# Expert blocks of 32 slots, four side by side, in a two-layer diffusion backbone on one NeuronCore

## The reference

```python
scores = jax.nn.sigmoid(jnp.dot(t, router_w))          # 16 experts in 4 groups
sel = scores + router_b                                # group of the best two sums, then top 2 inside it
a = jnp.einsum('td,edf->tef', t, w_gate)               # (1024 -> 256) per expert
b = jnp.einsum('td,edf->tef', t, w_up)
act = jax.nn.silu(a) * b * gates[:, :, None]           # gates: the two normalised scores, 0 elsewhere
return jnp.einsum('tef,efd->td', act, w_down)          # (256 -> 1024)
```

## Time and profile before

| | |
|---|---|
| Runs | 1114.5, 1116.32, 1115.82 us; median 1115.82 |
| Profiled execution | span 1112.5 us from first to last instruction; no time of its own beside the span |
| TensorE | busy 1058.8 us, 95% of the span |
| VectorE, ScalarE, GpSimd | 572.7, 389.0, 204.8 us |
| DMA | 241.47 MB, mean 217 GB/s |

### The profile page before, as it was taken

The page is one execution under the profiler, slowest core; times in us unless marked ns, Lnnn a source line. Parts: engine busy times, 40 slices in busy tenths (PEclk is TensorE's granted clock), DMA queues, the critical chain, the costliest instruction groups (busy, mean ns, idle before and its releaser), DMA issues.

```text
span 1112.5 us, 17990 instructions
## 1 busy us (share of the span) xinstructions
PE 1058.8 (95%) x5918; PEld 589.1 (53%) x5919; DVE 572.7 (51%) x1223; ACT 389.0 (35%) x800; POOL 204.8 (18%) x313
## 2 busy tenths in 40 slices
PE   3999999999999899999999999899999979999996
PEld 0566564555544455555546655555644445555552
DVE  0334545665345754454574545476724674534557
ACT  0332224444211244444333222454511134444540
POOL 0133456000000100100152435800000011001003
PEclk9999999999999999999999999999999999999999
DMA  9940006668801799999981000557540379999917
GB/s 351 361 138 1 1 9 238 217 222 302 331 19 40 248 378 377 381 358 366 332 289 41 1 1 0 187 194 279 207 149 38 112 260 376 381 379 380 376 78 284
DMA packets 129064, 241.47 MB, mean 217 GB/s; under 512 B 12304, under 2 KB 92192, under 8 KB 122864
## 3 DMA queue, kind: packets, MB, share of 16 engines
q1 hardware_dynamic: 115904, 194.83, 50.1%
q0 software_dynamic: 7056, 25.69, 6.3%
q10 hardware_dynamic: 6048, 20.22, 4.5%
HBM read 213.63 MB, written 27.10 MB: 216 GB/s over the span
## 4 chain that ended last, share of the span: by engine, by line
PE 80%; DMA 8%; DVE 3%; issue 3%; SPq 3%; POOL 1%; ACT 1%; DVEq 0%; POOLq 0%; ACTq 0%
PE bank L1120 17%; PE pair L1045 12%; PE pair L1160 9%; PE pair L762 7%; PE pair L777 6%; DMA big<-ada_w 4%; PE pair L895 4%; PE pair L794 3%; PE bank L811 3%; PE bank L931 3%; PE bank L672 3%; PE pair L1090 3%; PE bank L910 2%; PE bank L746 2%; DMA big<-y_rows,big 2%
## 5 line engine op out<-in xcount | busy, mean ns | idle before, releaser
L1120 PE MATMUL bank<-big,actT 128*64 (+1 forms) x928 | 206.3, 380 | 2.4 <-ACT actT L1445 1.9
L1120 PE MATMUL bank<-actT 128*64 128x256 f32 x928 | 206.5, 381 | 0.0
L1120 PEld LDWEIGHTS bank<-big,actT 128*64 128x64 f32 x928 | 124.7, 137 | 83.1 <-issue 26.0
L1045 PE MATMUL pair<-big,actT 128*128 128x512 f32 x320 | 142.7, 598 | 0.0
L1120 PEld LDWEIGHTS bank<-actT 128*64 128x64 f32 x928 | 124.7, 137 | 0.0
L1160 PE MATMUL pair<-big 128*64 (+1 forms) x464 | 106.0, 598 | 0.7 <-ACT big L1470 0.7
L1045 PEld LDWEIGHTS pair<-big,actT 128*128 128x128 f32 x320 | 59.0, 190 | 67.8 <-issue 67.6
L762 PE MATMUL pair<-big,actT 128*128 128x384 f32 (+1 forms) x320 | 93.6, 447 | 0.3 <-ACT actT L1218 0.2
L1988 DVE TENSOR_REDUCE mx<-pair 128x1 f32<-128x640 f32 x64 | 52.7, 823 | 72.0 <-PE pair L896 71.9
L1642 POOL DMA_INDIRECT big<-h_rows,big x29 | 27.7, 956 | 304.3 <-PE pair L1090 286.9
L762 PEld LDWEIGHTS pair<-big,actT 128*128 128x128 f32 x320 | 59.5, 190 | 29.3 <-ACT actT L1218 1.9
(11 more groups left out here) (274 smaller groups left out, 1628.9 us busy)
## 6 DMA issues: line engine op xcount, KB each, us to landing
big<-ada_w SPq DMA_DIRECT2D x48, 1024.0 KB, 5.0
big<-w_gate SPq DMA_DIRECT2D x32, 1024.0 KB, 13.1
big<-w_up SPq DMA_DIRECT2D x32, 1024.0 KB, 16.3
big<-w_down SPq DMA_DIRECT2D x32, 1024.0 KB, 14.5
y_rows<-big ACTq DMA_DIRECT2D x28, 512.0 KB
big<-w_out SPq DMA_DIRECT2D x4, 2048.0 KB, 13.4
big<-mod_rows SPq DMA_DIRECT2D x16, 512.0 KB, 9.2
h_rows<-big ACTq DMA_DIRECT2D x10, 512.0 KB, 2.7
```

The costliest lines, as they stand in the source:

```text
L1045: m = mm(dst, actT[:, k, t * P:(t + 1) * P], vw.wo[n][:, k, :], start=(k == order[0]), stop=(k == order[-1]))
L1120: m = mm(dst[CH * h:CH * h + CH, 0:DE], xgT[:, k, CH * h:CH * h + CH], weights(h, k * 2 * DE + lo, DE), start=(k == 0), stop=(k == DC - 1) ...
```

## The change

Blocks have 32 slots (`CH`), and four of them (`NPART`) stand side by side in a step, each on 32 columns of the array. Block 0 still reads the ring. Blocks 1 to 3 read copies, which now pass through queues of three pieces each: the 6144 columns of an expert are six pieces of 1024 (gate 0 and 1, up 2 and 3, down 4 and 5), and piece `i` of block `c` stands in `parts[c][i % 3]`. `ACT_TAKES` and `DVE_TAKES` say which engine copies which blocks of each piece. One semaphore, `used`, counts the pieces that TensorE is done with, and takes the place of `gu_mm` and `dn_mm`. Step 0 of a layer holds blocks of expert 0 alone and reads the ring for all four. The copies of pieces 0 to 2 of a step stand in the step before it, those of 3 to 5 in the step itself, so each engine reads places twice a step. Gate and up weights lie in the ring as runs of 8 KB (rows `8p` to `8p+7` in partition `p`), and so `norm2` writes its rows in the matching order. Every expert gets at least one block, expert 0 at least four. The SBUF set aside for DMA descriptors shrinks to 4096 bytes a partition.

```diff
-CH = 64
-NSTEP = 18
+CH = 32
+NPART = P // CH
+NSTEP = 15
+PIECE = D
+NPIECES = 6
+ACT_TAKES = [(1, 3), (1,), (1,), (1, 3), (1,), (1,)]
+DVE_TAKES = [(2,), (2, 3), (2, 3), (2,), (2, 3), (2, 3)]
...
+        fifo = sb("fifo", [P, 3 * PIECE])
...
-                    sp.dma_start(wgu[s][:, :, 0:DE], w_gate[l, e].rearrange("(k p) n -> p k n", p=P)).then_inc(ld_w[s], 16)
-                    sp.dma_start(wgu[s][:, :, DE:2 * DE], w_up[l, e].rearrange("(k p) n -> p k n", p=P)).then_inc(ld_w[s], 16)
+                    sp.dma_start(wg[s], w_gate[l, e].rearrange("(p k) n -> p (k n)", k=DC)).then_inc(ld_w[s], 16)
+                    sp.dma_start(wu[s], w_up[l, e].rearrange("(p k) n -> p (k n)", k=DC)).then_inc(ld_w[s], 16)
...
+                def weights_of(n, place, i):
+                    if n is not None:
+                        w_a, w_d = w_s
+                        pe.wait_ge(w_a, n * ACT_STEP + sum(len(t) for t in ACT_TAKES[:i + 1]) - 1)
+                        pe.wait_ge(w_d, n * DVE_STEP + sum(len(t) for t in DVE_TAKES[:i + 1]) - 1)
...
+                    for i in range(4):
+                        weights = weights_of(None if first else n, place, i)
+                        dst = (tb4, tb5)[i // 2]
+                        for k in range(4 * (i % 2), 4 * (i % 2) + 4):
+                            for c in range(NPART):
+                                m = mm(dst[CH * c:CH * c + CH, 0:DE], xgT[:, k, CH * c:CH * c + CH],
+                                       weights(c, k % 4 * DE, DE), start=(k == 0), stop=(k == DC - 1),
+                                       tile_position=(0, CH * c), skip_group_check=True)
+                        m.then_inc(used, 1)
```

ScalarE's part of a step:

```diff
+                    if not first:
+                        slot = part_place(n)
+                        part_copy_w(n, slot, 3)
+                    act.wait_ge(used, n * NPIECES + 4)
                     f(sil, tb4[:, 0:DE], ACT.Silu).then_inc(b_sil, 1)
+                    if not first:
+                        part_copy_w(n, slot, 4)
+                        part_copy_w(n, slot, 5)
                     for k in range(2):
                         act.wait_ge(b_at, n * 2 + (k + 1))
                         f(acT[:, k, :], (o6, a7)[k][:, 0:P], ACT.Copy).then_inc(b_atc, 1)
...
+                    rows_copy(n + 2)
+                    slot = part_place(n + 1)
+                    part_loaded(n + 1)
+                    for i in range(3):
+                        part_copy_w(n + 1, slot, i)
                     act.wait_ge(b_yd, n + 2)
                     act.dma_start(y_rows[bass.ds(n * P, P), :], yb).then_inc(b_st, 16)
```

In `norm2`:

```diff
-                    v.tensor_tensor(xn[t % 2], xn[t % 2], vw.S[:, c2, :], ALU.add).then_inc(h_ready, 1)
+                    v.tensor_tensor(h2, h2, plain(vw.S[:, c2, :]), ALU.add).then_inc(h_ready, 1)
...
```

VectorE's part of a step:

```diff
                     if last:
                         early_tables()
+                    if not first:
+                        slot = part_place(n)
+                        for i in range(3, NPIECES):
+                            part_copy_w(n, slot, i)
...
                     if not last:
                         rows_copy(n + 2)
-                        gu, down = half_weights(n + 1)
-                        gu(0).then_inc(w_d, 1)
-                        gu(1).then_inc(w_d, 1)
+                        slot = part_place(n + 1)
+                        part_loaded(n + 1)
+                        part_copy_w(n + 1, slot, 0)
                     ve.wait_ge(b_st, n * 16 + 16)
                     v.tensor_copy(is_ctx1, is_ctx[:, bass.ds(n, 1)]).then_inc(b_sel, 1)
                     ve.wait_ge(b_sel, n * 2 + 1)
                     stt(yb, gate[:, 0, :], is_ctx1, gate[:, 1, :], ALU.mult, ALU.add).then_inc(b_sel, 1)
...
                     if not last:
-                        down().then_inc(w_d, 1)
+                        part_copy_w(n + 1, slot, 1)
+                    ve.wait_ge(used, n * NPIECES + 8)
...
                     tt(yb, pair[1][:, :], yb, ALU.mult).then_inc(b_yd, 1)
+                    part_copy_w(n + 1, slot, 2)
...
+    nc = bacc.Bacc("TRN2", target_bir_lowering=False, num_devices=1, dynamic_dma_scratch_size=4096)
```

More of the change, by code:

```diff
@@ L52 @@
 HALF = 512
-CH = 64
-NSTEP = 18
+CH = 32
+NPART = P // CH
+NSTEP = 15
 NSTEP_MIN = 2 * NTOK // P
-NCHUNK = 2 * NSTEP
+NCHUNK = NPART * NSTEP
 NSLOT = NSTEP * P
 RING = 5
+PIECE = D
+NPIECES = 6
+ACT_TAKES = [(1, 3), (1,), (1,), (1, 3), (1,), (1,)]
+DVE_TAKES = [(2,), (2, 3), (2, 3), (2,), (2, 3), (2, 3)]
+ACT_STEP, DVE_STEP = (sum(len(t) for t in takes) for takes in (ACT_TAKES, DVE_TAKES))
 EARLY = [[0, 1], list(range(NT))]
@@ L502, in load_layer @@
                     sp.wait_ge(b_st, n_steps * 16)
-                    sp.wait_ge(dn_mm, steps)
+                    sp.wait_ge(used, steps * NPIECES + 2)
                 sp.dma_start(vw.wukv[:, :, :], w_ukv[l].rearrange("(k p) n -> p k n", p=P)).then_inc(ld_ukv, 16)
@@ L1125, in products @@
+                def products(n, place, first):
                     pe.wait_ge(b_ta, n + 1)
                     pe.wait_ge(b_td, n + 1)
-                    pe.wait_ge(w_a, n * 3 + 1)
-                    pe.wait_ge(w_d, n * 3 + 1)
-                    gate_up(tb4, 0).then_inc(gu_mm, 1)
-                    pe.wait_ge(w_a, n * 3 + 2)
-                    pe.wait_ge(w_d, n * 3 + 2)
-                    gate_up(tb5, DE).then_inc(gu_mm, 1)
-                    return weights
-                def rest(n, last, weights):
-                    w_a, w_d = w_s
+                    for i in range(4):
[7 more added lines that the diff above has]
+                        m.then_inc(used, 1)
@@ L1139, in turn_act, with rest @@
+                def rest(n, place, first, last):
                     def turn_act(k):
@@ L1170, in _ @@
                 n_more = pe.value_load(n_more_s[0:1, 0:1], min_val=NSTEP_MIN - 1, max_val=NSTEP - 1)
-                rest(0, False, weights)
+                rest(0, place_0, True, False)
                 def step(n, last):
-                    rest(n, last, products(n))
+                    place = load_place(n)
+                    products(n, place, False)
+                    rest(n, place, False, last)
                 with pe.Fori(1, n_more) as i:
```

208 lines of the change are left out of this document (100 added, 108 removed).

## The result

The changed kernel takes **1162.6 us** (median of 4 runs, 1158.6 to 1166.5), the kernel before 1116.1 (4 runs): ratio 1.041, 95% interval [1.038, 1.044]. The profiled execution has a span of 1162.1 us.

What follows compares the result with a forecast made beforehand. TensorE bounded the kernel before; afterwards a 15.2 us ring of copies and reads would. Span 1112.5 + 22.9 (steps) + 2.1 (last step) + 1 (norm2) = 1138.5, plus 3.3 gives 1141.8 us; range 1108 to 1160.

Steps and rivals of the forecast that it cites:

- Fewer steps: Expert stages: 25 steps for 29, worth 4 x 12.1 = 48.4 us at an unchanged step.
- TensorE's work in a step: Four 32-column products take nearly the time of two 64-column ones; TensorE keeps its 12.1 us a step: 0.
- The ring: Chain through VectorE, ScalarE's store, reads and piece 3 copies, and TensorE: 15.2 us a step, +22.9 us in all.
- R: The start of VectorE's rows' copy, from which the times round a step's ring are counted.
- ScalarE from y to its copies: Ring link: wait for y, store issue and loop turn 0.68, two reads 1.2, wait and address: 2.2 us.
- A quarter off: Reads and waits a quarter off either way: steps of 14.4 to 16.0 us, 18 us either way in total.
- The 3.3 us that were added from span to median: Kernel before: median 1115.8 us lies 3.3 above profiled span 1112.5; the same 3.3 was added to the forecast span.
- Rival A's 14.0: Reads hide under work in flight; ring without ScalarE's 1.2 us of reads is 14.0 us, total 1114; chance 0.10.
- The last step: early_tables stand ahead of VectorE's piece 3 copy: +2.1 us in layer 1, 0 in layer 0.
- The order of norm2: norm2 writes rows 128 elements apart: 0 to 1.3 us a layer, taken as 0.5, so +1 us.
- Runs of 8 KB: Gate and up weight loads: queue already moves 374 GB/s and TensorE doesn't wait for it; 0 either way.
- The range: Total time: likeliest forecast's own range 1124 to 1160 us; with rival A, 1108 to 1160.

Runs made afterwards that it cites:

- place_only: reads_between with VectorE's third read and five waits replaced by one semaphore wait, and TensorE's first read and five weight waits left out: 1096.2 us, 0.982.
- no_copies: Changed kernel without the weight copies of parts 1 to 3, their products taking rows of x; reads, waits and counts stay: 1107.0 us, 0.992.
- store_behind_copy: Changed kernel with ScalarE's wait for y and its store moved behind its two copies of piece 3: 1129.1 us, 1.011.
- one_more_read: Changed kernel with one more, unused, value read on ScalarE at the top of each step: 1190.3 us, 1.064.
- tables_late: Changed kernel with early_tables' products and sums in a layer's last step moved behind VectorE's activation products: 1163.9 us.
- reads_between: Changed kernel reading places once a step, store behind piece-3 copies, ScalarE reads earlier, VectorE reads between activation products and rows' copy, pieces 1, 2 copied earlier: 1100.0 us.

## Why the prediction came out too small

- **Fewer steps.** Right: 12 and 13 steps, 25 gathers. No kernel shows the whole 48 us; the kernel with the shortest steady steps, place_only, is 20 us below the one before.
- **TensorE's work in a step.** Right that four products of 32 columns run together: gate and up 6.74 us from first to last start, before 6.75; down 3.05 against 3.06. "TensorE keeps its 12.1" is right only while it waits for copies: its queue is through with the down product later than before and reads beyond its end, so that the floor was 12.5 (no_copies), 11.9 with one read (place_only).
- **The ring.** Right in kind: TensorE is idle ahead of pieces 0, 2 and 3, released by the copies named, and taking away either the reads or the wait for y shortens the step at once. Link by link, forecast and measured in the step shown: R to VectorE's first copy 3.2 and 3.16; to y 4.4 and 4.4; **ScalarE from y to its copies 2.2 and 2.8**; the copies 2.0 and 2.0; TensorE 2.0 and 2.2; to the next R 1.4 and 1.4. Sum 15.2 and 15.95, in the mean 15.83. **The step that failed first is the ring's third term, ScalarE from y to its copies:** 2.2 us forecast, 2.56 in the mean of 21 steps, the largest error in the ring. In the step shown the loop's turn takes 0.8 us with the issue (0.68 forecast) and the two reads 1.63 (1.2 forecast). They were priced at 0.59 us each by scaling VectorE's, a price at which the load instruction takes 0.28 us; in this place it takes 0.43 in the mean, and 0.65 and 0.39 in the step shown. The rows of before have no read so close behind a store, and in store_behind_copy, where the store stands behind them, the load instructions take 0.28 again (last section). Over 21 steps this term makes 8 us, TensorE's 0.2 us makes 3.5, and one step of 17.2 us in which VectorE's first copy waits for weights 1.7: 13 of the 23.5 us by which the span was missed.
- **The other 10 us** are terms that were put at nothing or too small: code ahead of the stage 3.7, between the layers 3.2, the last steps 2.9, the first steps 1.1, norm2 and tables 0.9, less 1.4 at the end. "A quarter off" in the reads was in the range (16.0 us a step); these terms pushed the time beyond it. The 3.3 us that were added from span to median are 0.5 in the changed kernel (1162.1 and 1162.6), which hid 2.8 us of the error: the median was missed by 20.8.
- **Rival A's 14.0,** the ring without ScalarE's reads, is what three kernels measured, but by luck: one of them has all the reads. In all three the ring through VectorE's copies of piece 2 closes at 14.0. The forecast's own terms have it (7.6 + 1.2 + 0.1 to piece 2, then half of gate and up and 1.4), and nobody added them up.
- **The last step.** 2.1 us forecast for the tables in layer 1; the gap ahead of piece 3 is 4.36 us and 2.1 in the other steps, as that implies, but TensorE's clock then fell (a mean of 0.75 from 1121.9 to 1142.0), which nothing in the sum had: with it the two last steps miss by 2.9 us.
- **The order of norm2.** 0.5 us a layer forecast, 0.71 measured between the two kernels. The other 0.25 us a layer that the stage grew are put down to the larger tables (0 forecast), which no run separates: 1.9 against 1. The row's write took 2.01 us and not 1.28, 1.57 times as long.
  The Trainium skill, "SBUF — State Buffer", section "Door 1: The DMA port swizzle", has a penalty for accesses that cross to ever new 16-byte lines. The trace agrees in kind, and a layer paid 0.7 us and not the 1.3 of a doubled operation.
- **Runs of 8 KB.** Costed at 0. On the kernel before this can't be judged; in the changed kernel going back to 1 KB costs 2.8 us in the first two steps of layer 0. The forecast had looked at the need of a steady step alone, and these two wait for weights in both kernels (TensorE 4.6 us with runs of 8 KB, 5.0 with 1 KB, and for the gather 1.3).
- **What was not looked at.** Between the layers the last y store takes 8.16 us to land; the next layer's w_uq is issued at 580.65, ahead of it (581.27), while before it was issued behind it (559.86 against 558.89). From the last transposes to layer 1's first is 2.6 us longer. No kernel was run to test that this order is the cause. The 3.7 us ahead of the changed stage are most likely no part of the change: the same code took 366.0 to 371.0 us in the thirteen executions of changed kernels that were profiled, and 367.3 in the one of before.
- **The range.** Its upper end came from the ring alone; that idle time may cost TensorE its clock as well had no place in it.

## What to carry to other kernels

A read of a value into a register stops its engine's queue for 0.6 to 0.8 us here: count reads per step, place each where the engine would wait anyway, and never behind a wait on a ring or right behind the issue of a store. When two edits each take the same link from a ring their gains do not add, and the next ring shows only then; adding up the second longest way round before the first run would have shown it here. Fed in the right order, blocks of 32 with all that came with them are worth 1.8% (place_only, 1096.2 against 1116.6 us), and after that late weights add to TensorE's time, above all in layer 0. No run tried the saved reads on the kernel with blocks of 64.

## What the runs showed of the hardware that was not expected

- TensorE can lose its clock over a gap inside a dense loop: after gaps of 2.5 to 4.4 us ahead of a piece the next quartets ran up to 0.43 us apart instead of 0.22 in 8 steps of one_more_read and in the last step of the changed kernel, and a step paid 1.4 us or more besides its gap. It need not: gaps of 2.7 us in four steps of one_more_read, 2.9 in a step of tables_late and 4.0 in the last step of reads_between left the products of piece 3 0.22 us apart.
- A read's load instruction is not of one length. On ScalarE it takes 0.28 us, but 0.27 to 0.99 us, 0.43 in the mean, where it stands behind the store, and steps of the same kernel differ by 0.7 us (15.5 to 16.2) with it. What the slow ones share is the y store. The fourteen traces have 2431 such reads on ScalarE and VectorE in the expert stages; the 199 whose load instruction takes over 0.35 us (up to 1.34, in no_copies) all start within 5.2 us of the issue of a y store, which takes 6.6 us to land in the changed kernel, and of the 1579 that start later none does. In store_behind_copy, where the edit puts ScalarE's reads 6.2 us and more behind the store, none takes over 0.33. The weight copies beside them are not the cause, since no_copies has none. How the store does it is open.
- In the kernel before TensorE's queue is through with the 16 down products 0.5 us after the first starts (481.24 to 481.75), and the loop's turn, its two reads and five waits, 3.0 us, end with the product. With 32 it takes 0.9 us (454.02 to 454.92 in no_copies) and the reads end at 457.99, 0.4 us too late.
